# Seven products of quarters for nearly all dense pieces and the output projections of a four-layer fp32 model

## The chip, the cores and the metric

The kernel runs on one core of a Trainium2 chip. The metric is the device time of one execution in microseconds (us). The kernel before was timed three times: 1535.61, 1532.9 and 1534.58 us, a median of 1534.58 us. All arithmetic is in fp32.

## The reference, cut to what matters

Two blocks run one after the other, each of two layers. The kernel calls the layers of the first block A0 and A1, those of the second B0 and B1. Widths: D = 1024; 256 tokens of `x` and, in the first block, 256 tokens of a context as well, so that A0 has 512 tokens and A1, B0 and B1 give results for 256.

```python
# A layer (twice): x and ctx
h = x * (1 + scale) + shift                     # scale, shift from silu(c) @ w_ada
parts = split(h @ w_in)                         # q,k,v,gate; gla q,k,v,decays,gate; sgu u,v,gate; 3 gates of 1024
y_attn = softmax(q k^T) v * silu(a_g)
y_gla  = chunked gated linear attention, both directions, * silu(g_g)
y_sgu  = s_u * (w_s @ layer_norm(s_v) + b) * silu(s_g)
m      = sigmoid(m_a)*(y_attn@w_br_attn) + sigmoid(m_g)*(y_gla@w_br_gla) + sigmoid(m_s)*(y_sgu@w_br_sgu)
x      = layer_norm(ALPHA * x + gate * (m @ w_out))

# B layer (twice): x only
h = rms_norm(x)
qkv, z_a, a, b, cf_val, cf_glu, z_b, gates = split(h @ w_in)
qkv = silu(depthwise_conv5(qkv)); o = gated delta rule, chunked, both directions
y_a = rms_norm(o) * silu(z_a) @ w_dn_out
y_b = silu(layer_norm(depthwise_conv31(cf_val * sigmoid(cf_glu)))) * silu(z_b) @ w_cf_out
x   = x + (sigmoid(g0) * y_a + sigmoid(g1) * y_b) @ w_out
```

## The kernel before

**Pieces and the ring.** A weight matrix is cut into pieces of 1024 rows and 512 columns (2 MB). SyncE loads them in one order, `PLAN` (`plan_a`, L55, `plan_b`), into a ring of seven units of 1 MB. A piece takes two units that follow one another, and its load waits until the tenants of these units have been used (`frees`). Where pieces are multiplied "by seven products" the ring is cut to its first four units, and the three others hold sums of weight quarters (`WW`), sums of token quarters (`HW`) and a scratch (`EW`).

**A dense piece, plainly.** `feat` (L861) makes four chunks of 128 features. Each is a sum over eight k of a 128x128 weight block (stationary) times all tokens (moving): 32 matmuls of 512 columns in A0 or 256 in A1 and B. `token` (L870) does the same with tokens stationary and 512 weight columns moving; the output projection `w_out` uses it. The profile counts two PE instructions for each such fp32 matmul.

**By seven products.** `WINOGRAD` (L47) holds a scheme by which a 2x2 block product takes seven products of quarters in place of eight: products 1, 2, 6, 7, 5, 4, 3. A product of a piece is two chunks by four k, with half the tokens moving (`one_of_seven`, L917). It needs four sums of weight quarters (128x1024 each, `seven_weights`, L1946), four sums of token quarters once a layer, copies of products 1, 6, 7, 5 from PSUM by ScalarE (`seven_copies`, L1469) and three sums of results (`seven_sums`, L1968). Before the change `SEVEN` (L52) names the pieces done so: in A0 gqk, gv, ag, gg, su; in A1 ag, gg, su, mg0, ms0, ma1. A0's five later gate pieces and the branch matrices beside them go by `seventh` and `later_piece` (L2208), with the weight sums on GpSimd. All pieces of B, sg, A0's ma0, A1's ma0 and mg1, and w_out in all four layers go plainly.

**Order.** Each engine runs its queue in order. Within a layer the three streams of work, dense pieces `d`, attention `a` and gated linear attention `g` in A (`ORDER_A`, L56), and dense `d`, delta rule and its merge `f` and the long convolution `c` in B (`ORDER_B`, L62), are interleaved by strings written out in the file, one letter a step. All engines follow the same string. After the string come in A the merge and w_out (`layer_a`: L1148 on TensorE, L2246 on VectorE), in B the second half of the merge and w_out (`layer_b`, L1432). In B the first half of the tokens of five chunks (`HALF_BANKS`) is multiplied ahead of the string.

**VectorE in B.** The delta rule (`delta`, L2359) makes 16 differences for the decays (128x128), the 5 taps of 12 chunks (12 of them first taps), a chain of some 60 small products and sums that inverts 16x16 blocks, and products of PSUM results. `conv` (L2322) makes 31 taps of 4 chunks, of which the first is a TENSOR_SCALAR. `tt`, `ts` and `stt` are helpers, so their instructions stand at L1927, L1930 and L1933; those of ScalarE's `copy` at L1459, those of TensorE at L850 (matmul) and L905 (transpose).

Of the kernel before, what the change touches and what calls it, by code (L numbers as in the profile page):

```python
# [1 line left out]

# [32 lines left out]
ADA_FIRST = [(0, 0), (0, 2), (0, 1), (0, 3)]  # L35
# [14 lines left out]
SEVEN = [[("gqk", "A"), ("gv", "A"), ("ag", "T"), ("gg", "T"), ("su", "A")],  # L50
         [("ag", "T"), ("gg", "T"), ("su", "A"), ("mg0", "G"), ("ms0", "G"), ("ma1", "G")]]
# [4 lines left out]
    "adddaddadddadddadaadddgagadaggadggdagddagaggaggadgagaddgaggdggdaaggdaaggaadadagagdgdaggagggdgaggdggaadaaggdaagda"  # L56
    "gagaagadagaagdggaagdagaagaggadaadaagadadaggaadaadadaagdagaadadgagaadaaddaggagadgaagdaadadaddagg",
    "dddaadaddaddgdgddadagddagdddaggadagdddagddagddgadgdgddaddgggdagdggdggdaagdaggadgdadaddggaadaggaadggdagddgaagdgad"
    "gddaaagdgagdadaaddgdgdgagadgggadaaggdggddgdgaggadgagdagdaggdaggaggggdg"]
ORDER_B = [  # L60
    "dfddddfdfdfffddfddfddffddfddffddffdfdfdffdcfdcdfdfccdcfdfdfdffdfcccfdccfcdfccfcffcdfdccfcffcdccfdfffffcfcfffccfc"
    "cdcfdcfcdcdffcfcfffffcdfffdcfdddffff",  # L62
    "dfddddfdfdfffddfdfdddffddfddfdfdffdfdfdffdfddcfdcfdcfdfdfdcffccccdcffdcccfcfcdfcfcfdfccfdccfcfdfcdcfcfffcffcffcc"
    "fcfcdcffdcddcfffcffffdfdfdddffffcfff"]


def plan_a(l):
    first = (("qa", 4096), ("kv", 8 * 288))
    out = [(f"a{l}{n}", w) for n, w in (first if l == 0 else first[::-1]) + (
        ("gqk", 4096), ("gv", 4096), ("ag", 4096), ("gg", 4096), ("su", 4096), ("sg", 4096), ("sv", 4096))]  # L70
# [28 lines left out]
def dense_a(l):  # L99
# [18 lines left out]
    for name, kind in (("gqk", "A"), ("gv", "A"), ("ag", "T"), ("gg", "T"), ("su", "A"), ("sg", "T")):  # L118
        steps += [[(name, c, kind)] for c in range(4)] + [ada()]
# [17 lines left out]

def act_events(n, x, kind):
# [3 lines left out]
    quarters = {7: ["t11"], 4: ["t22"], 3: ["t21"]}.get(x, []) if kind != "WA" else []  # L142
    return ([(n, x)] if x in (1, 6, 7, 5) else []) + [(n, t) for t in quarters] + ([(n, 3)] if x == 3 else [])


def dve_events(n, x, kind, first):
# [5 lines left out]
    gated = {7: ["g11"], 4: ["g22"], 3: ["g21", "g12"]}.get(x, []) if kind == "WT" else []  # L152
# [72 lines left out]
def build_program(nc, wf, consts, cT, xin, xinT, pa, ra, rpost, pb, rfin, out):  # L225
    with ExitStack() as ctx:
# [20 lines left out]
        XT0 = SB - 4096  # L247
# [24 lines left out]
        hT = r3(ma.take(4096), 8)  # L272
        qkv_gv = ma.take(5120)
# [27 lines left out]
        QB = [ma.take(512) for _ in range(2)]  # L301
# [6 lines left out]
        TM = mm_.take(512)  # L308
        mg_at = mm_.at
        zz, rp, gb, st6 = mm_.take(1024), mm_.take(2048), mm_.take(2048), mm_.take(16)  # L310
        XR = [mm_.take(1024) for _ in range(2)]
        xT = r3(arena[:, XT0:XT0 + 4096], 8)
# [23 lines left out]

        SPARE = [[X[:, 512 * c:512 * c + 512] for c in range(4)],
# [17 lines left out]
        THB, gh = mb.take(512), mb.take(16)  # L355
# [27 lines left out]
        for c in range(4):  # L383
            SIGB[(0, 0, c)], SIGB[(0, 1, c)], SIGB[(1, 0, c)] = SG0[:, c, :], CV[:, 4 + c, :], CV[:, 8 + c, :]
            SIGB[(1, 1, c)] = CU[:, c, 0:256]
        mo = Mem(arena, SB0)
        TMB, mTB = mo.take(256), r3(mo.take(2048), 8)
        fr, zzB, f2 = mo.take(1024), mo.take(1024), mo.take(4)
# [4 lines left out]
        def tiles(l):  # L393
# [26 lines left out]
        FIRST = [("pf", 0, "A"), ("pf", 1, "A"), ("ps", 0, "V"), ("ps", 1, "V"), ("pf", 2, "A"), ("pf", 3, "A"),  # L420
                 ("ps", 2, "V"), ("qh", 3, "-"), ("ps", 3, "V")]
# [19 lines left out]
        def seven_sum(l, n, s):  # L441
# [3 lines left out]
        ht_act, ht_dve, ht_pool, ht_pe = ev("ht_act", 4, 8), ev("ht_dve", 10, 8), ev("ht_pool", 2), ev("ht_pe", 0, 8)  # L445
# [22 lines left out]
        NOUT = [8, 4]  # L468
# [6 lines left out]
        ou_pe, ou_dve = ev("ou_pe", *NOUT), ev("ou_dve", *NOUT)  # L475
# [4 lines left out]
        DB = [("ab", 0)] + [(n, c) for n in ("q0", "q1", "q2", "za", "cv", "cg", "zb") for c in range(4)] + [  # L480
            (f"m{b}{j}", c) for j in range(2) for b in range(2) for c in range(4)]
# [3 lines left out]
        STT = [g for g in DB if g[0] in ("za", "cg", "zb")]  # L485
        db_pe, db_act, db_dve = ev("db_pe", 45, 45), ev("db_act", 45, 45), ev("db_dve", 12, 12)
# [19 lines left out]
        de_vh, de_sq, de_ss, de_ln, de_rn, de_nrm = (ev(n, k, k) for n, k in (  # L506
            ("de_vh", 1), ("de_sq", 2), ("de_ss", 8), ("de_ln", 4), ("de_rn", 2), ("de_nrm", 2)))
# [14 lines left out]
        ob_pe, ob_x = after(ou_pe, 4, 4), after(ou_dve, 4, 4)  # L522
        fn_sq, fn_ms, fn_rs, fn_x = (after(x, 0, 2) for x in (hb_act, hb_dve, hb_pool, cf_dve))
# [20 lines left out]
        for l in range(2):  # L544
# [4 lines left out]
            for n, i, kind in FLAT[l]:  # L549
# [5 lines left out]
                elif i == 1:  # L555
                    hold(("dense", l, n, 1), b, dense_dve(l, n, "g12") if kind == "WT" else dense_act(l, n, 3))
# [2377 lines left out]
```

## Time and profile before

| | |
|---|---|
| median of three runs | 1534.58 us |
| profiled execution: time, span | 1532.09 us, 1530.3 us |
| busy: PE, PEld, DVE, ACT, POOL | 97%, 73%, 49%, 28%, 19% of the span |
| granted TensorE clock, mean | 0.996 of full speed |
| chain that ended last, by engine | PE 89%, ACT 3%, DVE 3%, issue 2%, DMA 2%, POOL 1% |
| matmuls, instructions on PE | 8416 |
| read from HBM | 181.95 MB, mean 120 GB/s |

PE is TensorE's matmul, PEld its weight load, DVE VectorE, ACT ScalarE, POOL GpSimd. The layers lie in the span as follows, by where w_out ends: A0 to about 637 us, A1 to 989 us, B0 to 1256 us, B1 to 1523 us.

### The profile page before, as it was taken

What the parts mean: (1) busy time and instruction counts of PE and PEld (TensorE: products, weight loads), DVE (VectorE), ACT (ScalarE), POOL (GpSimd) and SP (SyncE); (2) the same over time, 40 slices, a digit from 0 to 9 for tenths busy, and PEclk for the clock granted to TensorE, in tenths of its full rate; (3) what the DMA queues carried; (4) which work ended last, traced back from release to release, by engine and by line L of the source; (5) the groups of instructions that cost most, each with busy time, mean ns of one, the idle gap of its engine ahead of it and who ended that gap; (6) DMA issues with size and microseconds to landing.
All of it is one profiled execution on the core that took longest, in us unless ns stands there. A gap on an engine that the chain in (4) does not pass through costs nothing.

```text
span 1530.3 us, 20417 instructions
## 1 busy us (share of the span) xinstructions
PE 1491.9 (97%) x8416; PEld 1123.3 (73%) x8416; DVE 755.5 (49%) x1546; ACT 429.2 (28%) x846; POOL 287.6 (19%) x314
## 2 busy tenths in 40 slices
PE   6999999999999999999999999999999999999997
PEld 2577776554788884655977988588888858888883
DVE  1266656642634333533745631356887215679621
ACT  1132454323121220122336330134333213423310
POOL 0223203200566441122111202110100011010010
PEclk9999999999999999999999999999999999999999
DMA  9542224300122213421332352533232233232221
GB/s 370 225 165 111 111 110 166 135 31 20 63 96 106 100 57 102 152 110 55 110 111 110 111 221 110 195 115 121 111 112 106 109 150 145 110 129 99 105 110 42
DMA packets 17376, 184.31 MB, mean 120 GB/s; under 512 B 2306, under 2 KB 2818, under 8 KB 4740
## 3 DMA queue, kind: packets, MB, share of 16 engines
q1 hardware_dynamic: 17284, 183.01, 31.3%
q8 instruction: 67, 1.10, 0.3%
q14 instruction: 25, 0.20, 0.0%
HBM read 181.95 MB, written 1.05 MB: 120 GB/s over the span
## 4 chain that ended last, share of the span: by engine, by line
PE 89%; ACT 3%; DVE 3%; issue 2%; DMA 2%; POOL 1%; SPq 0%; POOLq 0%; ACTq 0%; DVEq 0%
PE ps L850 85%; PE ps L905 3%; DVE arena L1933 2%; DMA arena<-in_wf 2%; POOL arena L2607 1%; DVE arena L1927 0%; ACT L1887 0%; ACT L1885 0%; ACT arena L1459 0%; DVE arena L2134 0%; DVE arena L1930 0%; ACT arena L1885 0%; ACT arena L1771 0%; ACT L1773 0%; ACT L1771 0%
## 5 line engine op out<-in xcount | busy, mean ns | idle before, releaser
L850 PE MATMUL ps<-arena 128*128 128x256 f32 (+9 forms) x7924 | 1443.6, 365 | 28.1 <-DMA arena<-in_wf 13.5
L850 PEld LDWEIGHTS ps<-arena 128*128 128x128 f32 (+5 forms) x7924 | 1070.2, 178 | 368.7 <-issue 236.4
L2607 POOL TENSOR_TENSOR arena<-arena 128x256 f32<-128x256 f32 (+6 forms) x254 | 254.5, 1021 | 808.9 <-DVE arena L1933 374.2
L1933 DVE SCALAR_TENSOR_TENSOR arena<-arena 128x256 f32<-128x256 f32 (+4 forms) x482 | 237.8, 544 | 115.1 <-ACT arena L1486 21.2
L1459 ACT ACTIVATE arena<-ps 128x512 f32<-128x512 f32 (+3 forms) x312 | 148.9, 499 | 485.7 <-PE ps L850 410.6
L1927 DVE TENSOR_TENSOR arena<-arena 128x1024 f32<-128x1024 f32 (+12 forms) x253 | 205.8, 838 | 150.8 <-ACT arena L1459 83.2
L1927 DVE TENSOR_TENSOR arena<-ps,arena 128x512 f32<-128x512 f32 (+16 forms) x141 | 59.9, 449 | 123.8 <-PE ps L850 115.3
L1933 DVE SCALAR_TENSOR_TENSOR arena<-arena,ps 128x256 f32<-128x256 f32 (+2 forms) x109 | 47.2, 445 | 132.6 <-PE ps L850 90.7
L905 PEld LDWEIGHTS ps<-arena 128*128 128x128 f32 x488 | 55.8, 141 | 28.2 <-issue 18.3
L905 PE MATMUL ps<-arena 128*128 128x128 f32 x488 | 72.2, 278 | 1.3 <-DVE arena L1927 0.7
L1933 DVE SCALAR_TENSOR_TENSOR arena<-ps,arena 128x128 f32<-128x128 f32 (+2 forms) x86 | 30.8, 407 | 82.6 <-PE ps L850 82.2
L1930 DVE TENSOR_SCALAR arena<-arena 128x256 f32<-128x256 f32 (+9 forms) x181 | 62.8, 381 | 16.4 <-POOL arena L2607 10.8
L2611 POOL TENSOR_SCALAR arena<-arena 128x1 f32<-128x1 f32 (+2 forms) x22 | 14.7, 670 | 208.0 <-DVE arena L2047 81.3
L1737 ACT ACTIVATE arena<-ps,arena 128x256 f32<-128x256 f32 x32 | 14.9, 473 | 87.3 <-PE ps L850 82.1
L2179 DVE COPY_PREDICATED arena<-arena,ps 128x512 f32<-128x512 uint32 (+1 forms) x56 | 30.0, 589 | 5.0 <-PE ps L850 5.0
L2780 POOL TENSOR_SCALAR arena<-arena 128x128 f32<-128x128 f32 x16 | 11.4, 729 | 108.2 <-DVE arena L1933 108.2
L1590 ACT ACTIVATE arena<-ps,arena 128x512 f32<-128x512 f32 (+1 forms) x48 | 29.1, 615 | 5.4 <-DVE arena L1930 5.4
L2108 DVE TENSOR_REDUCE arena<-ps 128x1 f32<-128x512 f32 (+1 forms) x48 | 26.4, 591 | 4.5 <-PE ps L850 4.5
L1633 ACT ACTIVATE arena<-arena 128x1024 f32<-128x1024 f32 (+1 forms) x28 | 23.2, 840 | 1.5 <-POOL arena L2607 1.3
L1741 ACT ACTIVATE arena<-ps 128x256 f32<-128x256 f32 x24 | 9.1, 379 | 46.2 <-PE ps L850 46.2
L1896 ACT ACTIVATE arena<-arena 128x1024 f32<-128x1024 f32 x4 | 4.2, 1056 | 61.9 <-DVE arena L1933 61.9
L2072 DVE TENSOR_REDUCE arena<-arena 128x10 f32<-128x640 f32 (+1 forms) x8 | 5.4, 678 | 31.4 <-POOL arena L2607 31.2
(96 smaller groups left out, 308.2 us busy)
## 6 DMA issues: line engine op xcount, KB each, us to landing
arena<-in_wf SPq DMA_DIRECT2D x69, 2048.0 KB, 8.0
arena<-in_wf SPq DMA_DIRECT2D x22, 1024.0 KB, 7.8
arena<-in_wf SPq DMA_DIRECT2D x2, 1152.0 KB, 7.7
arena<-in_xinT SPq DMA_DIRECT2D x2, 1024.0 KB, 16.0
arena<-in_xin SPq DMA_DIRECT2D x4, 512.0 KB, 3.8
arena<-in_rp SPq DMA_DIRECT2D x2, 1024.0 KB, 8.4
arena<-in_consts SPq DMA_DIRECT2D x1, 1410.0 KB, 21.1
arena<-in_pa SPq DMA_DIRECT2D x2, 532.0 KB, 9.8
```

The costliest lines, as they stand in the source:

```text
L850: return e.matmul(o, l, r, start=start, stop=stop, skip_group_check=True)
L905: return e.transpose(b[:, 128 * i:128 * i + rows], x, ident[0:rows, 0:rows])
L1459: return e.activation(o, i, ACT.Copy, **kw)
L1590: e.activation(Pb[h][:, 0:L], psum("att", l, "s", 2 * w + h)[:, 0:L], ACT.Exp, bias=sm[:, 1, h:h + 1], scale=0.125, accum_out=sm[:, 2, h:h ...
L1633: e.activation(x, x, ACT.Exp, scale=1.0 / 16).then_inc(gl_fe.hit(l, 7 * hp + n), 1)
L1737: ins = e.activation(SIGB[(j, bi, c)], x, ACT.Tanh, scale=0.5, bias=gh[:, q:q + 1])
L1927: return e.tensor_tensor(o, x, y, op)
L1930: return e.tensor_scalar(o, x, s1, None, op0) if s2 is None else e.tensor_scalar(o, x, s1, s2, op0, op1)
L1933: return e.scalar_tensor_tensor(out=o, in0=x, scalar=s, in1=y, op0=op0, op1=op1)
L2108: ins = e.reduce_max(sm[:, 0, h:h + 1], psum("att", l, "s", 2 * w + h)[:, 0:L], AX)
L2179: e.copy_predicated(att[:, tl[0]:4, h, :], both(2 ** n).unsqueeze(1).to_broadcast([128, nt, 128]), r3(psum("gla", l, "l", k)[:, L0:512], n ...
L2607: return e.tensor_tensor(o, x, y, op)
```

## The change

1. `SEVEN` grows: A0 gets sg and ma0, A1 gets sg, ma0 and mg1. In B ten of eleven pieces go by seven products (`SEVEN_B`; only q0 and the small ab stay plain), each product with 128 tokens moving, with weight sums, token sums and result sums on VectorE. Their ring is four units (two pieces) from q1 to m11, units 4 to 6 hold the sums.
2. w_out goes by seven products in all layers: 14 products for a pair of token tiles, each of 4 matmuls (8 PE instructions) of 256 columns, in the order `OUT_ORDER`. The first two need only the first half of the merged rows.
3. Some of VectorE's work in B goes to ScalarE: the first taps of both convolutions, the 16 differences of the decays (as Relu with a bias), eight scalings for the state (`KG`), the squares of the normalisation. Halvings are folded into weights and scales.
4. The start: the first piece of `w_ada`, the input and q's weights come in five slices of the k dimension (1, 1, 2, 2, 2 of 8 blocks), and q's products follow slice by slice.
5. The last norm goes by quarters and four output DMAs; some scratch tiles of the merge are doubled; the table loads at the delta rule's end are grouped; all four order strings are new, and za comes after cg.

```diff
-SEVEN = [[("gqk", "A"), ("gv", "A"), ("ag", "T"), ("gg", "T"), ("su", "A")],
-         [("ag", "T"), ("gg", "T"), ("su", "A"), ("mg0", "G"), ("ms0", "G"), ("ma1", "G")]]
+SEVEN = [[("gqk", "A"), ("gv", "A"), ("ag", "T"), ("gg", "T"), ("sg", "T"), ("su", "M"), ("ma0", "G")],
+         [("ag", "T"), ("gg", "T"), ("sg", "T"), ("su", "M"), ("ma0", "G"), ("mg0", "G"), ("ms0", "G"), ("ma1", "G"),
+          ("mg1", "G")]]
+OUT_ORDER = [(0, 1), (1, 1), (0, 2), (0, 7), (0, 6), (0, 4), (1, 7), (1, 2), (1, 6), (1, 4), (0, 5), (1, 5), (0, 3), (1, 3)]
+SEVEN_B = ["q1", "q2", "cv", "cg", "za", "zb", "m00", "m10", "m01", "m11"]
+def dense_b_steps():
+    steps = [[("ab", 0)]] + [[("q0", c)] for c in range(4)]
+    for n in SEVEN_B:
+        steps[-1] = steps[-1] + [("w1", n)]
...
+        steps.append([(n, 1), (n, 2), ("w2", n)] + late + ([("g2", last)] if last in GATED_B else []))
+        steps.append([(n, 6), (n, 7)] + ([("g1", last)] if last in GATED_B else []))
+        steps.append([(n, 5), (n, 4)] + ([("hz", last)] if last == "za" else []))
+        steps.append([(n, 3)] + ([("h2", n)] if n[0] == "m" or n in GATED_B else []))
...
+            def seven_b(l, n, x):
...
+                p.wait_ge(db_copied(l, n, {6: 1, 5: 6, 4: 7, 3: 5}[x]))
+                if len(s) == 1:
+                    p.wait_ge(db_added(l, n, "w" + s))
...
+                for c in range(2):
+                    for k in range(4):
+                        ins = mm(b[:, 128 * c:128 * c + 128], W[:, k, 128 * c:128 * c + 128], H[:, k, :],
+                                 x in (1, 2, 7) and c == k == 0, k == 3)
...
+            def seven_weights_b(l, n, first):
...
+                def make(s, x, y, op, product):
+                    if product:
+                        v.wait_ge(*([db_done(l, SEVEN_B[k - 1], product)] if k else rest_free[2 + l]))
+                    tt(w21 if s == "1" else WWB[s], x, y, op).then_inc(db_dve.hit(l, DB_DVE[(n, "w" + s)]), 1)
+                if first:
+                    v.wait_ge(pieces[f"b{l}{n}"][2])
+                    make("3", w11, w21, ALU.subtract, 7)
+                    v.wait_ge(db_added(l, n, "w3"))
+                    make("2", w22, WWB["3"], ALU.subtract, 6)
...
+            def out_product(l, j, x):
...
+                for k in range(4):
+                    ins = mm(b[:, 0:256], H[:, k, :], W[:, k, :], x in (1, 2, 7) and k == 0, k == 3)
```

## Rows read from the trace of the kernel before

**Rows 1.** The page: busy time of each engine, and the 40 slices

```profile
PE 1491.9 (97%) x8416; PEld 1123.3 (73%) x8416; DVE 755.5 (49%) x1546; ACT 429.2 (28%) x846; POOL 287.6 (19%) x314
...
PE   6999999999999999999999999999999999999997
DVE  1266656642634333533745631356887215679621
```

**Rows 2.** Waits of PE: for what, total us, times, longest

```profile
PE ps L850 <- DMA arena<-in_wf: 13.5, 4, 9.2
PE ps L850 <- issue: 4.1, 4, 2.5
```

**Rows 3.** Busy time by stretch: length, PE, PEld, DVE, ACT, POOL, clock, DMA share, GB/s

```profile
116.00:372.00 256.00, 255.06 (x1393) 168.32 (x1392) 144.43 (x268) 98.82 (x194) 48.46 (x67) 1.00 0.26 99
372.00:581.00 209.00, 206.88 (x925) 171.81 (x923) 86.70 (x81) 43.38 (x71) 103.46 (x56) 1.00 0.22 85
714.00:900.00 186.00, 185.98 (x1308) 152.10 (x1307) 105.47 (x203) 70.47 (x157) 29.80 (x58) 1.00 0.32 120
1005.00:1215.00 210.00, 206.72 (x1548) 181.28 (x1547) 139.66 (x386) 71.53 (x145) 12.19 (x11) 1.00 0.28 102
```

**Rows 4.** Timeline of PE: start us, us, what, output<-input form, count

```profile
861.51 20.37 PE L850 MATMUL ps<-arena 128*128 128x128 f32 x180
...
1020.34 45.06 PE L850 MATMUL ps<-arena 128*128 128x256 f32 x208
```

**Rows 5.** Timeline of PE at w_out of A0, of A1 and of B0; idle before in brackets

```profile
581.42 19.12 PE L850 MATMUL ps<-arena 128*128 128x512 f32 x44 [2.54 <-issue]
...
961.67 27.70 PE L850 MATMUL ps<-arena 128*128 128x512 f32 x64 [0.54 <-issue]
...
1228.37 20.84 PE L850 MATMUL ps<-arena 128*128 128x512 f32 x48 [1.36 <-DVE arena L1933]
```

**Rows 6.** The page: PE's weight loads, busy and mean ns

```profile
L850 PEld LDWEIGHTS ps<-arena 128*128 128x128 f32 (+5 forms) x7924 | 1070.2, 178 | 368.7 <-issue 236.4
```

**Rows 7.** Groups by form on VectorE in 990 to 1228 us: busy us, mean ns

```profile
L1933 DVE SCALAR_TENSOR_TENSOR arena<-arena,ps 128x256 f32<-128x256 f32 x24 | 10.0, 419 | 27.9 <-PE ps L850 22.9 <-ACT arena L1741 5.0
L1930 DVE TENSOR_SCALAR arena<-arena 128x256 f32<-128x256 f32 x24 | 9.8, 455 | 0.0
...
L1930 DVE TENSOR_SCALAR arena<-ps,arena 128x128 f32<-128x128 f32 x16 | 4.3, 341 | 5.0 <-PE ps L905 5.0
...
L1927 DVE TENSOR_TENSOR arena<-arena 128x512 f32<-128x512 f32 x4 | 2.7, 705 | 0.3 <-ACT arena L1459 0.3
L1927 DVE TENSOR_TENSOR arena<-arena 128x1024 f32<-128x1024 f32 x2 | 2.4, 1224 | 8.1 <-ACT arena L1759 6.4 <-ACT arena L1459 1.7
...
L1930 DVE TENSOR_SCALAR arena<-arena 128x128 f32<-128x128 f32 x8 | 1.7, 280 | 0.7 <-PE ps L850 0.7
```

**Rows 8.** Busy time in three stretches of B0, columns as in Rows 3

```profile
1080.00:1095.00 15.00, 15.00 (x80) 13.38 (x79) 14.83 (x47) 4.88 (x11) 5.72 (x8) 1.00 0.18 61
1080.00:1170.00 90.00, 89.15 (x956) 78.05 (x955) 74.73 (x228) 25.58 (x60) 7.53 (x9) 1.00 0.25 96
1200.00:1215.00 15.00, 15.00 (x72) 13.19 (x71) 3.03 (x7) 1.90 (x4) 0.00 (x0) 1.00 0.08 17
```

**Rows 9.** The start: two stretches, columns as in Rows 3

```profile
0.00:20.00 20.00, 7.38 (x42) 1.97 (x43) 3.83 (x13) 3.78 (x6) 0.86 (x5) 1.00 0.91 363
20.00:42.00 22.00, 20.73 (x74) 8.03 (x73) 2.32 (x10) 2.29 (x4) 0.69 (x1) 0.92 0.82 329
```

**Rows 10.** Timeline of PE and SyncE's issues at the start

```profile
1.15 0.42 SPq L790 DMA_DIRECT2D arena<-in_wf  x1
...
9.21 3.60 PE L850 MATMUL ps<-arena 128*2 128x512 f32 x16 [9.21 <-DMA arena<-in_wf]
...
35.90 3.60 PE L850 MATMUL ps<-arena 128*128 128x512 f32 x8
...
41.20 31.66 PE L850 MATMUL ps<-arena 128*128 128x512 f32 x128 [1.27 <-ACT arena L1665]
```

**Rows 11.** The page: weight loads of 2 MB, median us to landing

```profile
arena<-in_wf SPq DMA_DIRECT2D x69, 2048.0 KB, 8.0
```

**Rows 12.** The chain that ended last, near 100 us: start us, us, what

```profile
99.98 7.92 DMA arena<-in_wf
107.92 1.24 DVE arena L1927
```

**Rows 13.** Timeline of the end

```profile
1522.82 0.69 DVE L1933 SCALAR_TENSOR_TENSOR arena<-ps,arena 128x512 f32<-128x512 f32 x1 [6.17 <-PE ps L850]
1523.54 1.06 ACT L1911 ACTIVATE arena<-arena 128x1024 f32<-128x1024 f32 x1 [12.59 <-DVE arena L1933]
...
1525.94 1.28 DVE L1933 SCALAR_TENSOR_TENSOR arena<-arena 128x1024 f32<-128x1024 f32 x1 [1.06 <-POOL arena L2607]
```

More of the change, by code:

```diff
@@ L1 @@
 from contextlib import ExitStack
+from itertools import chain
 import numpy as np
@@ L300, in build_program @@
         KDT = [attf[:, 0:512], attf[:, 512:1024]]
-        QB = [ma.take(512) for _ in range(2)]
+        qb = ma.take(1024)
+        QB = [qb[:, 0:512], qb[:, 512:1024]]
         ST = ma.take(1024).rearrange("p (d n v) -> p d n v", d=2, n=4)
@@ L335, in build_program @@
         assert rest.at <= NU * UNIT
+        rest = Mem(arena, 4 * UNIT)
+        HWB = {n: r3(rest.take(512), 4) for n in "1234"}
+        WWB = {n: r3(rest.take(1024), 4) for n in "234"}
+        EWB, THR = r3(rest.take(256), 2), rest.take(512)
+        assert rest.at <= NU * UNIT
         SPARE = [[X[:, 512 * c:512 * c + 512] for c in range(4)],
@@ L1868, in delta @@
                 copy(Y64[:, 0:8, :], r3(psum("y", l, 4, 0), 8)).then_inc(de_yc.hit(l, 4), 1)
+                a.wait_ge(de_ga.at(l, GA_EXP + 3), de_tmc.at(l, 3))
+                for q in (1, 2):
+                    for i in range(4):
+                        o = 4 * q + i
+                        t, h = (o // 4) % 2, o % 4
+                        ins = copy(KG[:, o, :], K3[:, t, 128 * h:128 * h + 128], scale=BC[:, 32 + o:33 + o])
+                    ins.then_inc(de_kg.hit(l, q - 1), 1)
                 yield
@@ L2335, in conv @@
+                            if i == 30 and c == pair[1]:
+                                ins.then_inc(cf_dve.hit(l, CF_CONV + n), 1)
+                            else:
+                                ins.then_inc(v.own(), 1)
+                                last[c] = v.now()
                         if i % 2 == 0:
                             yield
-                    for c in pair:
-                        v.wait_ge(last[c])
-                        ins = ts(CA[:, c, :], CA[:, c, :], 0.5, parB[:, PB_FB + c:PB_FB + c + 1], ALU.mult, ALU.add)
@@ new lines, in layer_b @@
+                for n, _ in enumerate(merge(l, 1)):
+                    if n in (9, 11):
+                        next(sums)
+                out_sums = chain(out_token_sums(l), sums)
+                next(out_sums)
+                next(out_sums)
+                for i, (j, x) in enumerate(OUT_ORDER):
+                    t, f = OUT_PART[x]
+                    o = X[:, 1024 * t + 512 * j + 256 * f:1024 * t + 512 * j + 256 * f + 256]
+                    v.wait_ge(ob_pe.at(l, i), out_added(l, j, {2: 1, 4: 6, 5: 7}[x]) if x in (2, 4, 5) else None)
+                    stt(o, psum("ou", 2 + l, j, {2: 2, 7: 7, 4: 7}.get(x, 1))[:, 0:256], 0.5, o, ALU.mult, ALU.add
+                        ).then_inc(ob_x.hit(l, i), 1)
+                    next(out_sums, None)
+                    if l and i in (10, 13):
+                        last_norm(i == 13)
@@ L2847 @@
     pieces = {}
+    for n, (a, b) in enumerate(ADA_FIRST):
+        w = I["w_ada"][0]
+        pieces[f"a0f{n}"] = lay(np.concatenate([w[:, o + 128 * a:o + 128 * b] for o in (0, 1024)], 1))
     for l in range(2):
```

976 lines of the change are left out of this document (630 added, 346 removed).

## Prediction

> **What bounds the kernel now.** I read the page's busy shares first, then its slices, then the waits of PE, then the stretches by stage. PE is busy 97% of the span, and 9 in every slice but the first and the last [rows 1]. Its longest waits are for weights at the start and some four "issue" gaps of 4.1 us in all [rows 2]. So the time is TensorE's work plus some 20 us at the start, at the joints and at the end. The stretches show who comes next: in B0's interleaved part, 1005 to 1215 us, VectorE is busy 139.7 of 210 us (67%), in A0's 144.4 of 256 (56%), in A1's 105.5 of 186 (57%), ScalarE and GpSimd far less [rows 3]. The change takes matmuls away and gives VectorE sums, so the question is whether B still ends with TensorE.
>
> The sum is made against the profiled execution, 1532.1 us (span 1530.3 and 1.8 around it), 2.5 us under the median of 1534.6. The runs of before lie within 2.7 us of each other, so I call anything within 0.2% (3 us) no change.
>
> **TensorE's part.** Pace of one PE instruction, from long unbroken runs: 256 columns 45.06 / 208 = 0.216 us, 128 columns 20.37 / 180 = 0.113 us [rows 4], 512 columns 27.70 / 64 = 0.433 us [rows 5].
> - A piece of 256 tokens: 64 x 0.216 = 13.8 us now; by seven 7 x 16 = 112 instructions of 128 columns, 12.6 us. Less 1.2. There are 10 in B0, 10 in B1, 3 in A1: 23 x 1.2 = 28 us.
> - A piece of 512 tokens: 64 x 0.433 = 27.7; by seven 112 x 0.216 = 24.2. Less 3.5, twice in A0 (sg, ma0): 7 us.
> - w_out: 27.7 for two token tiles; by seven 14 x 8 = 112 x 0.216 = 24.2. Less 3.5, five times (A0 has two pairs): 17.6 us.
>
> Together 53 us, 10 of the 63 that one eighth would give being lost because 128 columns cost more than half of 256.
>
> Here a rule counts against the change. The trace's 128 columns go at 0.113 us [rows 4]. The Trainium skill ("TensorE: Matmul & The Clock Gate", Back-to-back issue gap) says that the spacing of short matmuls is set by the weight load as well, and gives 81 ns for 128 columns where the isolated gap is 56. By that ratio a 128-column instruction would take about 0.155 us, a seven-product piece 17 us, and 23 pieces would lose some 80 us (an estimate from that page). The trace disagrees for fp32: 180 in a row kept 0.113. Without the page: PEld's busy time per instruction is 1070.2 / 7924 = 0.135 us [rows 6]; if new operands made that the pace, a piece would take 15.1 us and the 23 pieces would cost 2.5 us each more than in my sum, +58 us.
>
> **The start.** PE worked 7.4 of the first 20 us and 20.7 of the next 22, 14 us lost [rows 9]. The first product waited until 9.2 for 2 MB; the second half of q began at 41.2, 5.3 us after the last `w_ada` product of the first stage at 35.9, and holds 32 instructions of 0.43, so q ends near 55 [rows 10]. After: slices; the last needs 12 MB, at the 363 GB/s of [rows 9] 33 us plus 1.2 until the first issue is out [rows 10], then about 2 us of products, the same 5.3 us of round trip (under which q's slice before runs) and q's last quarter, 6.9 us: about 48. Gain 6 us; ends 0 (DMA serves the slices no earlier) and 11 (nearly all the loss of the first 20 us goes). I take 6, since the bytes are the same.
>
> **Joints and end.** w_out waited 2.5 us in A0, 0.5 in A1, 1.4 in B0 [rows 5] and I count the same 1.4 for B1, for the last merged rows; now its first two products need only half the rows. 5.8 us in all; I take 3, the rest being the token sums (0.7 us each, [rows 7]) that the third product on waits for; ends 0 and 6. The end: a 512-column sum 0.7, square 1.1, scale by 1.3 us [rows 13] go by quarters and halves: -1, ends -2 and 0.
>
> TensorE's sum: 1532.1 - 53 - 6 - 3 - 1 = 1469.
>
> **VectorE in B.** What is added in each B layer [rows 7]: 40 weight sums x 1.22 = 49, 30 result sums x 0.42 = 12.6, 4 token sums x 0.7 = 2.8: 64 us. What goes to ScalarE or is folded away: 16 differences 4.3, 20 TENSOR_SCALARs of 256 at 9.8 / 24 = 0.41, 8.2; eight scalings 1.7; one halving of 0.7; about 2.3 in the norm and gates (three instructions of some 0.7): 17 us. So 139.7 + 64 - 17 = 187 us of VectorE beside 206.7 + 3.3 waiting = 210 less 12.5 = 197.5 us of TensorE. In the last steps (m11 and four merge products, some 16 us) VectorE has little: 3 us in 15 now [rows 8], about 5.5 then. Ahead of them it is 182 us of VectorE in 181.5 us: full to the brim. Any time that VectorE must then wait in its queue, for a product, a ScalarE copy or its own chain, TensorE waits too, because product 6 of the next piece waits for the second weight sum, and that one stands behind everything of the steps before.
>
> How well is VectorE filled? Best slice 14.83 of 15 us; the busy stretch 1080 to 1170, where taps fill the delta rule's chain, 74.7 of 90 (83%), but there it was waiting for a TensorE that was full [rows 8]. So the fill lies between 0.83 and 0.99, and I take 0.94, above the middle, as a queue that is behind finds its operands ready. Then 182 / 0.94 = 193.6, plus 16, is 209.6: 12 us over TensorE's 197.5, hardly less than the 210 of now. At 0.99: +2. At 0.83: 219 + 16, +38 a layer. Two layers: +24 (from +4 to +76).
>
> ScalarE takes over 16 + 16 + 8 small instructions, at 0.4 us some 16 us on top of 71.5 in 210: hidden. Its four copies of a piece replace four of before.
>
> **VectorE in A.** A0 gets two pieces (4 x 1.22 + 3 x 0.7 = 7 us each) and four gatings for su, about 17 us on 144 in 256; A1 three (4.9 + 1.3 = 6.2 each) on 105 in 186: at 65 to 70%, hidden by TensorE. w_out's sums: per pair of tiles ten result operations of 0.42, four token sums of 0.7 and the old work; 8 weight sums, 9.8 us, go beside the merge, where VectorE has 87 of 209 us [rows 3]. I allow 3 us for local stalls, ends 0 and 15.
>
> Forecast: 1469 + 24 + 3 = 1496 us.
>
> **Rivals.**
> 1. VectorE doesn't bind: the new orders fill it to 0.99 and the taps lie in all gaps. For it: slice 14.83 of 15. Against it: 182 us in 181.5. Then 1469 + 4 + 0 = 1473.
> 2. VectorE becomes the bound of B at the fill that the trace shows over 90 us, 0.83. Place: q1 to m01 in both B layers; price +38 each. 1469 + 76 + 3 = 1548, slower than before. It decides from where both layers together give back all 60 us that the rest saves: 211.5 us of string after the last steps, a fill of 0.86 and less. For it: the delta rule's chain needs round trips over PE and ScalarE, and seven-product sums wait in order for products; against it: taps are independent and there are 120 of them.
> 3. Weights come late. With four units a piece of B loads only when the last but one is used, m11 only after m01; in A0, sv now waits for su, and gv's load after gqk shows what that costs: the chain stood on DMA for 7.9 us and then on a weight sum of 1.24 [rows 12]. A load takes 8.0 [rows 11]. If sv, B0's m11 and B1's m11 each find only 3 of the 8 us covered: +15, 1511. Against it: the new strings put a dozen delta and merge steps ahead of m11.
> 4. 128-column products at the pace of the weight loads: 1496 + 58 = 1554, slower. The 180 in a row speak against it.
>
> **Chances.** Forecast 45%, rival 1 25%, rival 3 14%, rival 2 12%, rival 4 1%, and 3% for sums that end within 0.2%. Faster: 45 + 25 + 14 = 84%; same 3%; slower 13%. The range reaches down to rival 1 with little more (1470) and up past rival 3 to the turning point, 1535: it leaves out rival 2, rival 4 and a few per cent below.
>
> **What would show it.** After the change: 20 x 112 instructions of 128 columns in B at 0.113, w_out in 24.2 us a pair; first product by 7 us, q done by 49; VectorE above 85% in B's strings, and waits of PE for L-numbers of VectorE's sums of 10 to 15 us a layer, where now there are almost none. If PE's waits in B stay under 3 us a layer, rival 1 was right; if they pass 30, rival 2; if they are for DMA, rival 3. The forecast is wrong if B0's string is under 200 or over 220 us long.

## The result and the profile after

The changed kernel takes 1496.28 us (median of 4 runs, 1494.06 to 1498.38) beside 1534.36 for the kernel before (4 runs): ratio 0.9758, 95% interval 0.9743 to 0.9773. Two more sets of runs of the unchanged changed kernel, taken with the experiments, gave 1496.03 and 1496.24. The forecast was 1496, range 1470 to 1535.

(A correction to the description of the kernel before: in its file `WINOGRAD` stands at L45, `SEVEN` at L50, `ORDER_A` at L55, `ORDER_B` at L60 and `plan_a` at L67.)

The page of the changed kernel: busy time of each engine and the slices, to be set beside [rows 1].

```profile
PE 1445.5 (97%) x9872; PEld 1206.5 (81%) x9872; DVE 936.4 (63%) x1727; ACT 498.4 (33%) x1053; POOL 308.6 (21%) x316
...
PE   7999999999999999999999999899998999999998
...
DVE  1366666664544357623757744559999555999946
```

TensorE's share of the span is still 97%, with 1456 instructions more and 46.4 us less of busy time. VectorE has 181 us more, and its row now has two blocks of 9, the full stretches of B0 (slices of 1009 to 1158 us) and B1. TensorE's row has three 8s: the joint between A1 and B0 (934 to 971 us), B0 at 1121 to 1158, and the end.

TensorE's waits over the whole run (what it waited for: us, times, longest), beside [rows 2]:

```profile
PE ps L989 <- DVE arena L2194: 12.3, 12, 3.5
PE ps L989 <- DMA arena<-in_wf: 7.5, 2, 6.2
PE ps L989 <- ACT arena L1662: 7.4, 8, 2.4
```

Weights cost it 13.5 us before and 7.5 now. VectorE is now the first thing it waits for. Stretches of B0 in the changed kernel, columns as in [rows 3]:

```profile
990.00:1157.00 167.00, 157.25 (x1775) 152.21 (x1776) 161.00 (x369) 78.29 (x186) 14.62 (x11) 1.00 0.33 120
990.00:1050.00 60.00, 58.31 (x514) 57.53 (x514) 54.91 (x105) 25.55 (x75) 4.73 (x2) 1.00 0.46 167
1050.00:1150.00 100.00, 95.46 (x1241) 92.14 (x1242) 99.09 (x249) 47.87 (x104) 9.89 (x9) 1.00 0.25 91
1157.00:1235.00 78.00, 77.93 (x444) 70.32 (x444) 40.61 (x70) 18.19 (x39) 11.09 (x20) 0.98 0.42 158
```

Up to 1157 us VectorE is busy 161.0 of 167 us, over 100 us of that 99.1. Behind 1157 it has 40.6 us in 78 and TensorE stands for nothing. TensorE's timeline in the full stretch, the idle time before a row in brackets:

```profile
1023.84 12.77 PE L989 MATMUL ps<-arena 128*128 128x128 f32 x112 [0.48 <-DVE arena L2194]
1037.17 12.77 PE L989 MATMUL ps<-arena 128*128 128x128 f32 x112 [0.56 <-DVE arena L2194]
...
1062.60 2.05 PE L989 MATMUL ps<-arena 128*128 128x128 f32 x16 [2.13 <-ACT arena L1662]
...
1156.82 68.30 PE L989 MATMUL ps<-arena 128*128 128x256 f32 x360 [3.52 <-DVE arena L2194]
```

A piece by seven is 112 instructions in 12.77 us, 0.114 us each, the pace of [rows 4]. About half a us of waiting for VectorE stands before some pieces, and there are two larger pauses of 2.1 and 3.5 us.

**Where the 36 us came from.** Five places can be found in both traces, by instructions that the change leaves alone: the transposes near the end of q's part, the transposes just before w_out of A0 and of A1, and the decay's transposes at the start of B0 and of B1 (L1232 before, L1417 after). The forecast column splits the sum on record over the same segments.

| segment | before, us | after, us | difference | forecast |
|---|---|---|---|---|
| start, to 72.80 / 68.44 | 72.8 | 68.4 | -4.4 | -6 |
| A0, to 576.97 / 565.08 | 504.2 | 496.6 | -7.5 | -7 |
| A0's w_out and A1, to 960.10 / 936.87 | 383.1 | 371.8 | -11.3 | -12 |
| A1's w_out and the joint, to 1011.42 / 990.55 | 51.3 | 53.7 | +2.4 | -4 |
| B0, to 1276.93 / 1247.69 | 265.5 | 257.1 | -8.4 | -4.7 |
| B1 and the end, to 1530.3 / 1494.3 | 253.4 | 246.6 | -6.8 | -5.7 |
| stalls allowed in A | | | | +3 |

(The column adds up to -36.4: for a B layer the prediction takes 12.5 us off TensorE in its VectorE paragraph and 12 in its sum, and by its own paces ten pieces give 11.8.) The sum was met to the microsecond by errors that cancel, and that is luck: the joint from A1 to B0 came out 6 us worse than forecast, the B layers 5 better, and the 3 us of stalls in A didn't come.

### The profile page after: what moved, and what is told of

Its sections match the earlier page's. It is cut to its first block, busy times and chain, and to the rows that moved or that the text cites. A ratio compares the mean times of both kernels' runs of the same rounds, so it can differ in the third digit from the quotient of the medians.

```text
span 1494.3 us, 23877 instructions
## 1 busy us (share of the span) xinstructions
PE 1445.5 (97%) x9872; PEld 1206.5 (81%) x9872; DVE 936.4 (63%) x1727; ACT 498.4 (33%) x1053; POOL 308.6 (21%) x316
## 4 chain that ended last, share of the span: by engine, by line
PE 77%; DVE 16%; ACT 3%; issue 2%; DMA 2%; POOL 0%; SPq 0%; DVEq 0%; POOLq 0%; ACTq 0%
PE ps L989 73%; DVE arena L2200 9%; DVE arena L2194 6%; PE ps L1044 4%; DMA arena<-in_wf 1%; DMA arena<-in_rp 1%; ACT arena L1662 0%; ACT arena L2068 0%; DVE arena L2416 0%; DVE arena L2895 0%; POOL arena L3032 0%; ACT arena L2073 0%; DVE arena L2615 0%; ACT arena L1692 0%; POOL arena L3028 0%
## 5 line engine op out<-in xcount | busy, mean ns | idle before, releaser
L989 PE MATMUL ps<-arena 128*128 128x128 f32 (+8 forms) x9380 | 1394.2, 329 | 32.6 <-DVE arena L2194 12.3
L989 PEld LDWEIGHTS ps<-arena 128*128 128x128 f32 (+5 forms) x9380 | 1153.3, 181 | 246.5 <-issue 129.2
L2194 DVE TENSOR_TENSOR arena<-arena 128x1024 f32<-128x1024 f32 (+11 forms) x454 | 411.5, 929 | 187.7 <-ACT arena L1662 107.7
L3028 POOL TENSOR_TENSOR arena<-arena 128x256 f32<-128x256 f32 (+6 forms) x254 | 270.6, 1086 | 852.7 <-DVE arena L2200 293.2
L1662 ACT ACTIVATE arena<-ps 128x256 f32<-128x256 f32 (+2 forms) x427 | 193.9, 469 | 697.6 <-PE ps L989 641.4
L2200 DVE SCALAR_TENSOR_TENSOR arena<-arena 128x256 f32<-128x256 f32 (+4 forms) x492 | 236.2, 535 | 73.8 <-ACT arena L1692 24.3
L2194 DVE TENSOR_TENSOR arena<-ps,arena 128x256 f32<-128x256 f32 (+16 forms) x201 | 84.0, 436 | 96.3 <-PE ps L989 84.3
L2200 DVE SCALAR_TENSOR_TENSOR arena<-arena,ps 128x256 f32<-128x256 f32 (+2 forms) x87 | 36.8, 442 | 57.8 <-PE ps L989 51.0
L2200 DVE SCALAR_TENSOR_TENSOR arena<-ps,arena 128x128 f32<-128x128 f32 (+2 forms) x106 | 37.0, 390 | 24.9 <-PE ps L989 24.8
L2197 DVE TENSOR_SCALAR arena<-arena 128x512 f32<-128x512 f32 (+8 forms) x121 | 40.1, 356 | 13.6 <-POOL arena L3028 10.8
L1662 ACT ACTIVATE arena<-arena 128x512 f32<-128x512 f32 (+3 forms) x72 | 34.1, 527 | 5.2 <-POOL arena L3028 4.0
L1692 ACT ACTIVATE arena<-arena 128x256 f32<-128x256 f32 (+1 forms) x36 | 17.5, 485 | 31.4 <-PE ps L989 20.2
L1839 ACT ACTIVATE arena<-arena 128x1024 f32<-128x1024 f32 (+1 forms) x28 | 23.3, 840 | 10.4 <-PE ps L989 6.3
## 6 DMA issues: line engine op xcount, KB each, us to landing
arena<-in_consts SPq DMA_DIRECT2D x1, 1410.0 KB, 22.4
```

The costliest lines, as they stand in the source:

```text
L989: return e.matmul(o, l, r, start=start, stop=stop, skip_group_check=True)
L1662: return e.activation(o, i, ACT.Copy, **kw)
L1692: e.activation(o, src, ACT.Tanh, scale=0.5).then_inc(event("t" + q if q != "12" else 3), 1)
L1839: e.activation(x, x, ACT.Exp, scale=1.0 / 16).then_inc(gl_fe.hit(l, 7 * hp + n), 1)
L2194: return e.tensor_tensor(o, x, y, op)
L2197: return e.tensor_scalar(o, x, s1, None, op0) if s2 is None else e.tensor_scalar(o, x, s1, s2, op0, op1)
```

## The experiments

Each was run beside the kernel before, whose median was 1533.3 to 1533.9 in all three sets of runs. Differences below are to 1496.2, the middle of the three medians of the changed kernel. The executions of the unchanged changed kernel lie between 1494.1 and 1498.8 us, so I take a median as good to about 1 us and don't tell a difference of less than 2 us from none. The set with the cut sums, all ten pieces plain, m01 plain and the earlier fetch had no runs of the unchanged changed kernel beside it.

**All of VectorE's weight sums in B cut short.** In `seven_weights_b`:

```diff
-                    tt(w21 if s == "1" else WWB[s], x, y, op)...
+                    o, x, y = ((w21 if s == "1" else WWB[s])[:, :, 0:8], x[:, :, 0:8], y[:, :, 0:8])
+                    tt(o, x, y, op)...
```

This leaves out 31/32 of each sum (8 of a quarter's 256 columns in each of its four k blocks), so the kernel no longer computes the model.

> Leaves out most of the weight sums of the ten pieces of the two B layers: each covers 8 columns of a quarter in place of 128, all waits and products stay. My theory, that in a B layer VectorE (96 per cent busy over the first 167 us of B0) sets the pace of the first pieces: its 40 weight sums a layer fall from about 0.55 us to about 0.1, TensorE's waits for it in B0 and B1 (6.3 us in B0) and what stands behind them go, 1496.3 falls to about 1480 (1476 to 1486). Rival, that what is lost in B is ScalarE's copies, the weights' arrival or the matmuls' own pace: 1492 to 1497.

Measured: 1489.08 us (1488.28 to 1490.14), ratio 0.9709 [0.9695, 0.9723]: -7.2, half of what I expected, and between my range and the rival's. VectorE's busy time fell by 77.5 us. (The expectation has a sum's size wrong: it spans 256 columns and takes 1.22 us, and the cut one 0.23.) The stretch 990 to 1157 us of this kernel:

```profile
990.00:1157.00 167.00, 159.24 (x1789) 154.43 (x1787) 129.49 (x376) 77.88 (x185) 13.23 (x11) 1.00 0.34 127
```

And from its timeline of TensorE, the first merge product:

```profile
1152.87 3.69 PE L989 MATMUL ps<-arena 128*128 128x256 f32 x16 [3.19 <-DVE arena L2194]
```

VectorE went from 161.0 to 129.5 us in 167, and TensorE still did only 2 us more work in them. B0 took 253.6 us (989.7 to 1243.3) in place of 257.1. So VectorE's weight sums cost about 3.5 us a layer, not the 7 to 8 that I read into the waits: the larger part of these waits, 3.2 us before the first merge product and 2.1 for a ScalarE copy that stands behind two table loads and six activations, is there with VectorE busy 78% of the stretch too. This run doesn't show what the rest of VectorE's load costs.

**All ten B pieces plain.** `SEVEN_B`'s pieces by four plain halves each, copied by ScalarE, without sums:

```diff
+PLAIN_B = ["q1", "q2", "cv", "cg", "za", "zb", "m00", "m10", "m01", "m11"]
...
+                            feat(bank("db", l, n, x), use(f"b{l}{n}", 8), 128 * c, hB, 0, 256)...
```

> All ten dense pieces of both B layers by plain matmuls again (the four halves of a piece copied by ScalarE, no weight sums there); everything else as after. By my own terms for the first B pieces: the before kernel had six or so of them plain; the matmuls that come back are at least 12.5 us a layer, VectorE's waits of some 8 us a layer go: theory 1505 (1500 to 1511). Rival, that the products save their full price and VectorE costs nothing: 1521 (1516 to 1526). Rival that VectorE eats all of it: 1496 or less.

Measured: 1504.28 us (1502.86 to 1505.01), ratio 0.9807 [0.9793, 0.9821]: +8.1 as expected. (The expectation's words on six plain pieces before are wrong: before, all were plain; the sum in it doesn't use that.)

```profile
990.00:1157.00 167.00, 163.40 (x1323) 143.75 (x1323) 101.85 (x287) 68.66 (x168) 12.62 (x11) 1.00 0.30 113
```

B0 takes 264.8 us here. With products by seven and the cut sums it was 253.6, so there ten pieces are worth 11.2 us, 1.1 each, where I had 1.2. With the real sums it is 257.1: by seven the B pieces bring 7.7 us in B0, 11.2 less the 3.5 that the weight sums take back. B1 with the end gives less: 248.8 us plain, 242.9 with the cut sums, 246.6 in the changed kernel, so 5.9 and 2.2. Over the whole kernel TensorE's busy time with the cut sums is 24.8 us under the plain one's (1439.4 and 1464.2), 1.2 for each of the 20 pieces, but the medians are 15.2 apart, 0.8 for each: the work is saved as I had it, and a third of it is lost again in pauses and clock even with the sums cut.

**One piece plain, in two places.** m01 lies in the full stretch, m11 behind it. The edit is the one above with `PLAIN_B = ["m01"]` or `["m11"]`.

> One of the ten B pieces (m01, in the part where VectorE is fullest) by plain matmuls in both B layers. Theory (VectorE binds at that place): TensorE gains 1.2 us of work a layer, VectorE loses about 6 of its own, so the layer is 1 to 3 us shorter: 1491 to 1495. Rival (TensorE binds there too): 1.2 us a layer longer, 1498 to 1499.

> Only m11, the last of the ten B pieces, where VectorE has little to do, by plain matmuls. Theory (a piece by seven gives its 1.2 us only where VectorE has room): 1.2 a layer lost here, +2.4, where the same edit on m01, in the full part, moved nothing that could be told: +1.5 to +3.5 over the unchanged kernel of this call. Rival, that place doesn't matter: the same as m01, -2 to +0.5.

Measured: m01 plain 1494.56 us (1493.21 to 1495.63), ratio 0.9745 [0.9731, 0.9759]; m11 plain 1496.97 (1494.34 to 1498.63), 0.9768 [0.9749, 0.9787]. The first is -1.6, the second +0.8. The order is the one that the theory asks for, but neither differs from the changed kernel by more than can be told. By the traces B0 took 257.6 us with m01 plain (989.3 to 1246.9), so it isn't shorter there, and 259.3 with m11 plain (990.8 to 1250.1), 2.1 longer. That m01 by seven is worth about nothing where it stands agrees with both; it is not shown. What m01 plain does change is the pause before the first merge product, 1.25 us in place of 3.52, with two shorter ones behind it:

```profile
1154.29 3.69 PE L1007 MATMUL ps<-arena 128*128 128x256 f32 x16 [1.25 <-DVE arena L2226]
1158.95 3.72 PE L1007 MATMUL ps<-arena 128*128 128x256 f32 x16 [0.97 <-DVE arena L2232]
```

**More of VectorE in B.** The first weight sum of each B piece made twice:

```diff
+                    if s == "3":
+                        tt(WWB[s], x, y, op).then_inc(v.own(), 1)
+                        v.wait_ge(v.now())
                     tt(w21 if s == "1" else WWB[s], x, y, op)...
```

> The first weight sum of each B piece is computed twice (the same result written again), ten a layer, 1.22 us each: 12 us more of VectorE a layer, nothing else. Cutting 39 us of VectorE a layer gave 3.6 us in B0. Theory (at 96 per cent VectorE is at the edge: below it work is nearly free, above it every us counts, less what the first 60 us and m11 have room for): +6 to +10 a layer, 1508 to 1517. Rival (TensorE's waits in B are the delta rule's chain, not VectorE's queue): 0 to +5 in all, 1496 to 1501.

Measured: 1518.64 us (1518.02 to 1521.95), ratio 0.9918 [0.9901, 0.9936]: +22.4, above the range I gave, for 20 sums x 1.22 = 24.4 us of VectorE. B0 took 270.3 us (989.7 to 1260.1). The timeline of TensorE, the same two pieces as shown of the changed kernel:

```profile
1026.46 12.77 PE L989 MATMUL ps<-arena 128*128 128x128 f32 x112 [1.56 <-DVE arena L2194]
1041.06 12.77 PE L989 MATMUL ps<-arena 128*128 128x128 f32 x112 [1.83 <-DVE arena L2194]
```

TensorE's largest wait over the run:

```profile
PE ps L989 <- DVE arena L2194: 27.2, 20, 3.5
```

The pauses before a piece grew from 0.5 to 1.6 and 1.8, by 1.1 to 1.3 each: the length of the added sum. Its stretches:

```profile
1050.00:1150.00 100.00, 92.07 (x1171) 88.36 (x1170) 97.03 (x235) 47.09 (x105) 9.89 (x9) 0.95 0.28 104
1150.00:1170.00 20.00, 16.48 (x130) 15.16 (x130) 20.00 (x48) 7.62 (x12) 0.00 (x0) 0.98 0.19 66
```

With the cut sums this is a knee. Taking 77.5 us off VectorE gave 7.2 (0.09 us for each us), putting 24.4 on cost 22.4 (0.92 for each). Three points don't say where it bends: if a us costs 0.92 above the knee and nothing below, it lies 7.2 / 0.92 = 8 us, 4 a layer, under the changed kernel's load (an estimate). Nor do they part the amount from the place: the added sum stands directly ahead of the one that the next product waits for, and the same amount elsewhere in B was not tried. The same place in A is, next. Part of the price is the clock: 0.95 granted over 1050 to 1150, a mean between full speed and the lower of its two levels, 1.2 and 2.4 GHz, where it was 1.00 with the short pauses.

**More of VectorE in A.** The same doubling in `seven_weights`, for the 16 pieces by seven of A0 and A1:

> The first weight sum of each piece by seven in the A layers is computed twice (16 sums of 1.22 us, 19.5 us more of VectorE), as was done in B, where 24.4 us of VectorE cost 22.6. Theory, that VectorE is hidden in A (at about 65 per cent): 0 to +4, 1496 to 1500. Rival, that a sum in A delays its own piece's products, as the chain near 104 us has it: +10 to +20.

Measured: 1500.39 us (1499.5 to 1501.52), ratio 0.9782 [0.9768, 0.9795]: +4.2, just above the first range. The page shows the load on VectorE (956.4 us, 20 more):

```profile
PE 1447.7 (97%) x9872; PEld 1209.1 (81%) x9872; DVE 956.4 (64%) x1743; ACT 498.6 (33%) x1053; POOL 311.6 (21%) x316
```

0.2 us for each us, against 0.92 in B. Mostly hidden, as the fill of 56% in [rows 3] had it, but not wholly: TensorE's waits for L2194 rose from 12.3 to 16.8 us. My reading, not tried apart, is that a sum that its own piece waits for isn't hidden by the idle time elsewhere.

**w_out in B plain.** By four products of 512 columns for a pair of token tiles, as before:

```diff
-                for i, (j, x) in enumerate(OUT_ORDER):
-                    out_product(l, j, x).then_inc(ob_pe.hit(l, i), 1)
+                for i, (t, hf) in enumerate((t, hf) for t in range(2) for hf in range(2)):
+                    token(bank("ob", l, 2 + i), w, 512, mTB, 128 * t).then_inc(ob_pe.hit(l, i), 1)
```

> w_out of both B layers by plain matmuls of 512 columns again (64 in place of 112 of 256 for each pair of tiles), without its sums on VectorE. Theory, each w_out by seven is worth 64 x 0.433 - 112 x 0.217 = 3.4 us of TensorE and its sums lie beside: +6.8, 1503 (1501 to 1505). Rival, that the waits at its start and end eat half of it: +2 to +4.

Measured: 1502.36 us (1501.45 to 1504.33), ratio 0.9806 [0.9788, 0.9824]: +6.2 for two, 3.1 each where TensorE's work alone says 3.4. The term stands.

**The load at the joint.** TensorE's timeline between A1's w_out and B0 in the changed kernel:

```profile
937.74 24.34 PE L989 MATMUL ps<-arena 128*128 128x256 f32 x112
965.83 1.97 PE L1044 MATMUL ps<-arena 128*128 128x128 f32 x8 [3.75 <-ACT arena L1662]
968.27 11.19 PE L989 MATMUL ps<-arena 128*100 128x128 f32 x80 [0.47 <-ACT arena L1662]
```

VectorE's and SyncE's there:

```profile
949.68 0.79 SPq L934 DMA_DIRECT2D arena<-in_rp  x1
...
960.14 2.61 DVE L2200 SCALAR_TENSOR_TENSOR arena<-arena 128x1024 f32<-128x1024 f32 x2 [2.08 <-DMA arena<-in_rp]
```

w_out took 24.3 us in place of 27.7 [rows 5]. Then TensorE stood 3.75 us (0.9 at this place before), since the norm that feeds it waited 2.08 us for the parameters `rp`. SyncE issued their load only at 949.7, since in its queue it stands behind q0's, and that one waits for its buffers; 10.5 us later it had landed. The edit puts it ahead:

```diff
-            load("b0q0")
+            load("b0ab")
             s.wait_ge(gl_pr.end(1))
```

> In the second A layer SyncE issues the load of B0's parameters and residual (in_rp) ahead of the wait that holds it now. Theory, that the TensorE pause of 3.75 us between A1 and B0 comes from VectorE waiting 2.08 us for that transfer, and that the clock of 0.90 in the 23 us behind it comes with the pause: 1491 to 1494 (3 to 5 less). Rival, that something else (ScalarE's copies) ends the pause a moment later: under 1 us, 1495.5 to 1496.5.

Measured: 1493.61 us (1491.72 to 1495.3), ratio 0.9738 [0.9723, 0.9753]: -2.6. It is issued at 938.2. The same place on TensorE:

```profile
964.04 1.39 PE L1044 MATMUL ps<-arena 128*128 128x128 f32 x8 [2.60 <-ACT arena L1662]
```

And on VectorE:

```profile
959.67 1.28 DVE L2200 SCALAR_TENSOR_TENSOR arena<-arena 128x1024 f32<-128x1024 f32 x1 [0.92 <-POOL arena L3028]
```

The wait for the DMA is gone and the transposes start 1.8 us sooner, of which 1.2 are the pause. It is 2.60 us in all three traces with this edit (the two below have it too), and 3.6 to 4.1 in the ten without, so the cause of that part is shown. Of what is left of it at the decay's transposes behind the joint, nothing can be told: they start at 989.05 here, at 990.55 in the changed kernel, and at 988.8 to 991.3 in its two other traces and those of the B experiments, which are the same up to there. The traced execution is 4.7 us shorter than that of the changed kernel, but 3.2 of these lie in B1, which the edit leaves alone. The second half of my theory failed. 2.6 us of pause remain, the norm's own chain over GpSimd and ScalarE now that w_out ends sooner. And the clock behind it is about as low as before. The 24 us behind the joint in the changed kernel (the granted clock is the third number from the end):

```profile
966.00:990.00 24.00, 23.00 (x176) 22.20 (x176) 8.78 (x16) 10.94 (x25) 4.30 (x12) 0.86 0.00 1
```

And in this one:

```profile
966.00:990.00 24.00, 22.91 (x177) 22.50 (x178) 8.56 (x15) 9.52 (x20) 4.31 (x12) 0.88 0.05 11
```

**The norm's chain one step earlier.** The string of B0, and likewise that of B1, with the norm's products (an `f`) ahead of m01's products 5 and 4 (a `d`):

```diff
-    "cfdccfcccdfffcffc...
+    "cffdcccccdfffcffc...
```

> The earlier fetch of B0's parameters and residual, and in both B layers the two products of the norm (ms) one step earlier in the order, ahead of m01's products 5 and 4 in place of behind them. Theory, that the 3.5 us (B0) and 3.2 us (B1) for which TensorE stands before the first merge product are the norm's chain (square, ms, Ln, table load, Exp, two products on VectorE), begun a step late: each pause falls to about 1.3, another of 1.2 opens between the squares and ms, so 1 to 2 us a layer, with the fetch 1491 to 1494 (the unchanged kernel 1496). Rival, that VectorE's queue of taps sets the moment: no change beyond the fetch, 1493 to 1495, the pause still over 3.

Measured: 1497.58 us (1496.34 to 1502.46), ratio 0.9769 [0.9753, 0.9785], no gain, where the fetch alone gave -2.6, and above both ranges. Its trace is of the longest execution, 1502.46 us. The chain itself got shorter: from ScalarE's squares to its Exp it is 5.0 us (1148.23 to 1153.21) where it was 7.3 (1146.26 to 1153.55). But the rows of VectorE and TensorE before the first merge product are now:

```profile
1155.75 8.00 DVE L2200 SCALAR_TENSOR_TENSOR arena<-arena 128x256 f32<-128x256 f32 x20
...
1163.81 1.65 PE L989 MATMUL ps<-arena 128*128 128x256 f32 x3 [3.62 <-DVE arena L2200]
```

One letter moves every engine. Moving the `f` forward gathered five `c` in a row, 20 taps of the convolution, 8.0 us of VectorE, and its part of the next `f` stood behind them. The pause is still 3.6 us. So the edit didn't isolate the chain; what it shows is that in this stretch VectorE's queue decides, also over a pause that begins as a chain.

> The same, and m01 by plain matmuls in both B layers. Theory (TensorE and VectorE are balanced there, and m01 by seven is worth nothing): within 1.5 us of the kernel before it in this call, 1490 to 1494. Rival (by TensorE's work alone): 2.4 more than it.

Measured with m01 plain on top: 1497.14 us (1494.28 to 1498.78), ratio 0.9758 [0.9745, 0.9771], within 0.5 us of the one before, though both lie above the 1490 to 1494 that I gave. TensorE has 2.4 us more work and VectorE less, and the time is the same; the pause before the first merge product fell to 1.9 us.

**The best version.** The fetch alone (0.9738, 1493.6 us) is the fastest of all that leave nothing out, with m01 plain alone close by. It beats the kernel before by 40 us. Against the changed kernel it is 2.6 us better by the medians, but the intervals of the ratios overlap, and neither of the two runs with the fetch and the changed string was faster than the changed kernel. What is shown is a pause shorter by 1.2 us at the joint; a gain of 2.6 on the whole is not.

## Why the prediction was right, and where it wasn't

**TensorE's work, -53.** Right in kind and nearly in size. 128 columns kept 0.114 us in the new products, w_out took 24.3 us a pair. TensorE's busy time fell by 46.4 us. The mean granted clock fell from 0.996 to 0.992, and 0.4% of 1450 us is about 6 us (an estimate), so by it the matmuls were sized right and what is missing is clock, which my sum didn't have. In time a w_out in B is worth 3.1 us (3.5), and a B piece 0.8 (1.2) where VectorE is relieved of the weight sums: 1.1 in B0, 0.6 in B1. Rival 4, the pace of the weight loads, is excluded: a piece would have taken 15 us, and it took 12.8. The spacing of short matmuls of the Trainium skill ("TensorE: Matmul & The Clock Gate", Back-to-back issue gap), by whose ratio I had estimated 0.155 us, doesn't hold for these fp32 products.

**The start, -6.** The first product came at 6.21 us in place of 9.21 [rows 10]. TensorE's busy time in the first 20 us rose from 7.4 to 11.9 [rows 9]:

```profile
0.00:20.00 20.00, 11.88 (x48) 4.12 (x48) 2.47 (x11) 3.46 (x6) 0.20 (x4) 1.00 0.89 358
20.00:42.00 22.00, 21.52 (x93) 8.06 (x93) 3.48 (x15) 4.86 (x9) 0.00 (x0) 1.00 1.01 426
```

The gain at the end of this part was 4.4 us. I take the rate, 358 GB/s in the first 20 us beside 363 before, to be why not all of the loss could go; that was not tried. q's last products ended between 50 and 51 us, where I had 49.

**Joints, -3.** Wrong at one of them. I priced w_out's wait for the merged rows, and not what follows w_out: TensorE reached the next layer's transposes sooner, and the norm before them had lost its cover. A1 to B0 was 6 us worse than forecast: 3.75 us of pause where there had been 0.9, and the projections behind it took 11.2 us instead of 9.2 at a granted clock of 0.86 over 24 us, where the same work before had 1.00. The 2.08 us of waiting for `rp` are part of it: before, SyncE issued this load at 962.0, 0.4 us after w_out began, now 11.9 us after, since q0's load ahead of it is held until later in w_out. I had followed the order of SyncE's queue nowhere but at the weights. The step that failed is the sentence that takes 3 of 5.8 us as a gain; ends of 0 and 6 left no room for a loss.

**VectorE in B, +24.** The mechanism was right: it binds, and the experiment with more sums shows it at 0.92 us for each us. How large the loss is depends on what is counted. B's two strings, from the decay's transposes to w_out's first product (which I place by counting w_out's instructions back), in the changed kernel:

```profile
990.50:1202.50 212.00, 202.68 (x2030) 193.00 (x2031) 185.10 (x409) 89.71 (x209) 21.51 (x18) 0.99 0.36 132
1247.70:1464.10 216.40, 205.33 (x2031) 195.49 (x2032) 185.50 (x409) 89.80 (x209) 21.49 (x18) 0.98 0.34 127
```

Before, they took 217.0 us (1011.4 to 1228.4) and 218.2 (1276.9 to 1495.1). So they are 5.0 and 1.8 us shorter. TensorE's terms alone (12.5 for the pieces, 0.7 for w_out's wait) would have made it 13.2 each: 8.2 and 11.4 us were lost, 19.6 in all where I had 24. TensorE's busy time fell by 10.4 and 9.5 us, and its idle time grew by 5.4 and 7.7.

The weight sums account for 7.2 of these 19.6 us, by the run that cuts them, 3.5 a layer. The rest I had put down to VectorE's fill as well, and that step failed. It stays with VectorE at 78%: 2.1 us of waiting for the ScalarE copy, 3.2 before the merge, in B1 another 1.7 of "issue", and a granted clock of 0.98 over B1's string. How much of it hangs on the rest of VectorE's load is open. The pause before the merge shrinks to 1.25 us where m01 is plain, and that for the copy to 0.3 where all pieces are.

Of the fill itself, 0.94 wasn't far off (161.0 of 167 is 0.96), and neither was VectorE's total, 185 us a string where I had 187. The place was: I put 182 us ahead of the last 16 us of the string, and only 161 lie ahead of 1157 us, since m11 and its sums stand among the merges, behind the full stretch.

**Stalls in A, +3.** Not seen in the time: A0 and A1 came out at their sums (-7.5 and -11.3 against -7 and -12), though TensorE's waits for VectorE's helper `tt` up to B0 grew from 1.0 us (L1927) to 3.8 (L2194).

**The rivals and the signs.** Rival 1 (VectorE doesn't bind) is near the truth only for the weight sums, 3.5 us a layer beside its +2. B's strings lost 19.6 us where it had 4, and a further sum costs nearly its full length. TensorE's waits for VectorE's sums were 6.0 and 5.6 us a layer, between its 3 and the 10 to 15 that I gave. VectorE was busy 87% and 86% of the strings, as the signs asked. Rival 2, a fill of 0.83, isn't seen anywhere in B's full stretch. Rival 3, late weights in B: TensorE's two waits for weights, 7.5 us in all, both lie in A0 and at the start; in B there is none. (One reading at the prediction's start was short: TensorE stood for 38.4 us of the span before, not some 20. No sum uses it.)

## What to carry to other kernels

Where one engine is loaded to relieve another, find the amount at which they balance, and count only the work that must be done ahead of the point where the loaded one has slack again. Below that amount the load is nearly free (0.09 us for each us here), above it nearly full price (0.92), in these two runs, so cut or add a known amount before believing either. When a stage is shortened, price what comes right behind it: the chain that it used to cover, and the loads that are queued behind its buffers. And an order string that all engines follow can't move one engine's step alone.

## What the runs showed of the hardware

- VectorE's taps (128 x 256, fp32, from SBUF to SBUF) overlap. 180 instructions of this form in B0, most of them taps, have a mean of 473 ns and took 72.5 us, 0.40 us each:

```profile
L2200 DVE SCALAR_TENSOR_TENSOR arena<-arena 128x256 f32<-128x256 f32 x180 | 72.5, 473 | 0.0
```

  The Trainium skill ("VectorE: DVE Perf Modes", Two Vector instructions with no wait between them) says that a held instruction, by its model mostly one whose start quadrant differs from that of the last one to use the same memory, starts only when every earlier one has finished. These all work on 128 partitions, so none is such a case, and each starts on average 70 ns before the one ahead has ended (473 less 403); what a held one would cost, no run here shows.
- The clock behind a pause differs where the pause hardly does. Behind the 3.75 us at the joint the granted clock was 0.86 over 24 us (0.77 in the first 14 and 1.00 in the last 10), and 0.88 behind 2.60 us. Before, with 0.9 us of pause, it was 1.00. The traces of all runs have the same 80 projections behind this pause, 9.20 us long at full clock. Behind pauses of 3.6 to 4.1 us, in ten traces, they took 9.7 to 12.0 us, and behind 2.60, in three, 10.6 to 12.0. So from 2.6 to 4.1 us the length of the pause doesn't tell what is lost behind it; what does was not tried.
- Weights arrived at 426 GB/s between 20 and 42 us, against 329 in the same stretch before [rows 9], with the same 16 engines.
